# Output products with the tables stationary, and the stages behind the recurrence re-ordered, in a one-core trunk-and-MoE kernel

## What is computed

```
bu   = einsum(u, b)                      # u: tokens x 32 groups x 16 channels
h    = scan(a * h + bu)                  # complex, 64 states per group
y    = h_re @ c_re - h_im @ c_im + d * u # per group
y    = gelu(y);  y = y * sigmoid(y @ w_glu + b_glu)
mix  = concat([gated_mlp, y]) @ w_out;   x = x + gate1 * mix
h    = modulate(rms_norm(x));  group, expert = top-1 group, top-2 expert of h @ w_router
moe  = sum over the two experts of  gate * (silu(h @ w1) * (h @ w3)) @ w2
x    = x + gate2 * moe;                  out = rms_norm(x) * g_final
```

## Time and profile before

| what | us |
|---|---|
| median of three runs | 1870.66 |
| the profiled execution, its own time | 1870.08 |
| its span, first to last instruction | 1868.4 |

### The profile page before, as it was taken

How to read it: one execution, slowest core, us unless ns; L and a number is a source line. 1 busy time by engine, 2 the same in 40 slices (tenths; PEclk the granted TensorE clock), 3 DMA queues, 4 the chain that set the end, 5 groups by cost and what they waited for, 6 DMA issues and landing times. The chain is left out here.

```text
span 1868.4 us, 26204 instructions
## 1 busy us (share of the span) xinstructions
PE 1449.6 (78%) x6641; PEld 1086.6 (58%) x6642; DVE 1007.3 (54%) x2144; ACT 568.4 (30%) x976; POOL 701.0 (38%) x545
## 2 busy tenths in 40 slices
PE   3891899999859999398888886189999999994000
PEld 0140688888635666177777775168788887883000
DVE  3993756556355330335445553468555585761567
ACT  1121422323120000211111211068554485661232
POOL 0841223232115320023433333237443365563664
PEclk9996899999965555599999998589999999997555
DMA  4756311111181001634333342489976599985674
GB/s 117 267 181 219 113 68 45 67 57 61 36 164 40 18 6 69 233 115 166 136 135 135 149 149 73 155 276 372 359 270 244 207 370 363 325 313 184 215 276 161
DMA packets 165677, 322.78 MB, mean 173 GB/s; under 512 B 21677, under 2 KB 93421, under 8 KB 164952
## 3 DMA queue, kind: packets, MB, share of 16 engines
q1 hardware_dynamic: 150426, 276.20, 43.1%
q0 software_dynamic: 13664, 45.70, 7.1%
q10 hardware_dynamic: 1536, 0.26, 0.1%
HBM read 235.74 MB, written 86.39 MB: 172 GB/s over the span
## 5 line engine op out<-in xcount | busy, mean ns | idle before, releaser
L2022 POOL TENSOR_TENSOR down_lo<-expert_raw,down_hi (+1 forms) x64 | 157.1, 2476 | 180.9 <-ACT down_hi L2114 180.9
L2161 DVE TENSOR_TENSOR up_lo<-expert_raw,up_hi (+1 forms) x128 | 170.4, 1372 | 21.0 <-ACT up_hi L2109 20.2
L619 PE MATMUL ps_up<-up_hi,xT_hi 128*128 x400 | 161.8, 405 | 4.5 <-DVE up_lo L2161 2.9
L621 PE MATMUL ps_up<-up_hi,xT_lo 128*128 x400 | 157.2, 393 | 0.0
L620 PE MATMUL ps_up<-up_lo,xT_hi 128*128 x400 | 156.6, 392 | 0.0
L2109 ACT ACTIVATE up_hi<-expert_raw (+1 forms) x128 | 125.3, 1057 | 3.5 <-DMA expert_raw<-in_w 1.7
L619 PE MATMUL ps_out<-wout_hi,catT_hi 128*128 128x512 f32 (+1 forms) x272 | 109.0, 401 | 2.7 <-DVE catT_lo L1607 2.7
L621 PE MATMUL ps_out<-wout_hi,catT_lo 128*128 128x512 f32 (+1 forms) x272 | 107.5, 395 | 0.0
L620 PE MATMUL ps_out<-wout_lo,catT_hi 128*128 128x512 f32 (+1 forms) x272 | 107.4, 395 | 0.0
L448 PE MATMUL ps_ada<-wada,cT 128*9 128x512 f32 x192 | 87.7, 615 | 10.9 <-DMA wada<-in_w_ada 5.8
L782 POOL TENSOR_TENSOR v<-v,lng 128x512 f32<-128x512 f32 (+1 forms) x17 | 21.9, 1290 | 194.6 <-DVE v L931 194.6
(11 more groups left out here) (363 smaller groups left out, 3571.4 us busy)
## 6 DMA issues: line engine op xcount, KB each, us to landing
expert_raw<-in_w SPq DMA_DIRECT2D x96, 1024.0 KB
expert_rows<-yo SPq DMA_DIRECT2D x49, 512.0 KB
wada<-in_w_ada SPq DMA_DIRECT2D x12, 2048.0 KB
x<-in_x_prompt SPq DMA_DIRECT2D x32, 512.0 KB, 3.6
expert_rows<-blank SPq DMA_DIRECT2D x31, 512.0 KB, 4.1
x_rows<-x SPq DMA_DIRECT2D x16, 512.0 KB, 2.6
moe_in_rows<-h SPq DMA_DIRECT2D x16, 512.0 KB
x<-x_rows SPq DMA_DIRECT2D x16, 512.0 KB
```

The lines of the kernel that those rows point to most:

```text
L619: pe.matmul(out, left(0, k), right(0, k), start=k == 0, stop=False)
L621: last = pe.matmul(out, left(1, k), right(0, k), start=False, stop=k == n - 1)
L2022: pool.tensor_tensor(down_piece(down_lo, run, m), raw_piece(run, 2, m, 1), down_piece(down_hi, run, m).bitcast(F32), ALU.subtract).then_in ...
L2161: dve.tensor_tensor(up_piece(up_lo, run, m), raw_piece(run, m // 2, m % 2, KD // 2), up_piece(up_hi, run, m).bitcast(F32), ALU.subtract).t ...
```

## The change

`s5`. The output products swap their operands: the table is stationary and all 264 chunks of a group move, so a pair of groups takes six matmuls of 264 columns in place of what were, over the three sets of chunks, eighteen of 128. The result has steps and channels on the partitions; gelu writes it over the pair's inputs in `uT`; PE turns it back to token rows, four groups at a time and 128 chunks at a time, and ACT copies these. The sample chunks come first in `uT` now. Their outputs are gathered in one tile, turned, and stored with 32 small DMAs.

```
-                for m in range(4):
-                    for n in range(6 * m, 6 * m + 6):
-                        if m < 3 and n % 6 < 4:
-                            additions(4 * m + 4 + n % 6)
-                        outputs(n)
+                def outputs(k):
+                    if k == 0:
+                        pe.wait_ge(toep_in, 16 * Q)
+                    pe.wait_ge(h_ok, 2 * (k + 1))
+                    for g in range(2):
+                        if k > 0:
+                            pe.wait_ge(y_ok, 2 * (k - 1) + g + 1)
+                        pe.matmul(pB[:, g, 0:CH], toep[:, 2 * k + g, :], uT[:, 2 * k + g, :], start=True, stop=False)
+                    for h, m in ((h_re, S.m_re), (h_im, S.m_im)):
+                        for g in range(2):
+                            r = slice(g * ST, (g + 1) * ST)
+                            last = pe.matmul(pB[:, g, 0:CH], m[r, k, 1:9, :]..., h[r, k, 0:CH],
+                                             start=False, stop=h is h_im)
+                    last.then_inc(y_mm, 1)
+                def turn_back(m):
+                    pe.wait_ge(y_ok, 4 * m + 4)
+                    for t in range(2):
+                        if m > 0:
+                            pe.wait_ge(r_ok, 2 * (m - 1) + t + 1)
+                        for q in range(4):
+                            last = pe.transpose(pB[:, 2 + t, ...], uT[:, 4 * m + q, at[t]:at[t] + P], ident[:, :])
+                        last.then_inc(t_mm, 1)
+                for k in range(PAIRS):
+                    outputs(k)
+                    if k + 4 < PAIRS:
+                        additions(k + 4)
+                    if k >= 2 and k % 2 == 0:
+                        turn_back(k // 2 - 1)
+                turn_back(PAIRS // 2 - 1)
+                pe.wait_ge(y_ok, G + 1)
+                for i in range(2):
+                    pe.transpose(pB[:, i, 0:P], yT_samp[:, i * P:(i + 1) * P], ident[:, :]).then_inc(t_mm, 1)
...
+                for half in range(2):                       # SP
+                    cs = slice(half * DA // 2, (half + 1) * DA // 2)
+                    for t in range(2):
+                        sp.wait_ge(r_ok, 8 * half + 7 + t)
+                        sp.dma_start(y_rows[chunk[t]:chunk[t] + P, :, cs], rows[:, t, :, cs])
+                for i in range(2):
+                    sp.wait_ge(r_ok, PAIRS + i + 1)
+                    for g in range(G // 2):
+                        sp.dma_start(y_end[i, g, :, :, :], y_samp[g * NSEQ:(g + 1) * NSEQ, i, :]...)
...
+                for k in range(PAIRS):                      # ACT
+                    act.wait_ge(y_mm, k + 1)
+                    for g in range(2):
+                        act.activation(uT[:, 2 * k + g, :], pB[:, g, 0:CH], ACT.Gelu_apprx_tanh)
+                    if k >= 3 and k % 2 == 1:
+                        rows_back(k // 2 - 1)
```

```
@@ DVE step
                     if not last:
                         low_y(i + 1)
+                    if ranked:
+                        ranks(n - 2, 2)
                     gated(i, 0)
                     if not last:
                         bias_z(i + 1)
+                    if ranked:
+                        slots(n - 2, 2)
+                    if b == 1 and not (isinstance(n, int) and n == 0):
+                        select(n - 1, 2)
                     gated(i, 1)
-                    if b == 1 and not (isinstance(n, int) and n == 0):
-                        ranks(n - 1, 2)
...
-                    if b == 0 and not first:
-                        select(n - 1, 2)
-                    if b == 1 and not (isinstance(n, int) and n == 0):
-                        slots(n - 1, 2)
```

```
                     turn_x(b + 1, j + (t + 1) // AHEAD, (t + 1) % AHEAD)
+                    turn_hid(b - 1)
                     up_mm(b, t % 2, run_of(b))
                     down_mm(b - 1, run_of(b - 1))
-                    turn_hid(b)
```

```
                 def step(i, n, b):                          # POOL
-                    if within(i, NB - 1):
-                        if not (isinstance(i, int) and i == 0):
-                            pool.wait_ge(x_ok, i)
-                        gather(i + NB - 1, (b + NB - 1) % NB)
                     pool.wait_ge(two_ok, i + 1)
...
                     pool.tensor_tensor(yg[0:r, b, 1, :], yg[0:r, b, 1, :], g[0:r, :], ALU.mult)
+                    if i + AHEAD < NT:
+                        if i + AHEAD >= NB:
+                            pool.wait_ge(x_ok, i + AHEAD - NB + 1)
+                        gather(i + AHEAD)
```

More of the change, by code:

```diff
@@ L1075, in additions @@
                     last.then_inc(x_mm, 1)
[L1078 to L1082, removed]
-                        pe.wait_ge(toep_in, 16 * Q)
[L1084 to L1097, removed]
-                    last.then_inc(y_mm, 1)
@@ L1454, in step @@
                     if not first:
-                        logits(i - 1, NT if last else i + 2, n + b)
+                        logits(i - 1, NT if last else i + 2)
                 def rank(p, n):
@@ L1688, in step @@
                     first, last = isinstance(i, int) and i == 0, isinstance(i, int) and i == TP
+                    ranked = b == 0 and not (isinstance(n, int) and n < 2)
                     if last:
@@ L1704, in step @@
                         logits(i - 1, 1 - b)
+                    if last:
+                        select(7, 2)
                     dve.wait_ge(sq_ok, i + 1)
@@ L2156, in evac_x, with split_up @@
                                           xT_hi[:, par, ks, :].bitcast(F32), ALU.subtract).then_inc(x_d, 1)
-                def split_up(run, ms=range(4)):
-                    for m in ms:
+                def split_up(run):
+                    for m in range(4):
                         dve.wait_ge(up_h, 4 * run + m + 1)
@@ L2181, in step @@
                     evac_x(b + 1, prev)
[L2182 to L2187 removed]
+                    evac_hid(b - 1)
+                    split_next(dve, b, split_up)
+                    hidden(b, t % 2)
                     out(b - 1, AHEAD // 2 * j + (t - 1) // 2, prev)
[L2189 removed]
                 evac_x(0, 0)
@@ L2268, in step @@
                         sp.dma_start(o.y_prompt[0, ds(i * P, P), :], out[:, b, :]).then_inc(o_out[b], 16)
-                    if not isinstance(i, int) or i + NB < NT:
+                    if i + NB < NT:
                         load(i + NB, b)
-                tiles(sp, step)
+                tiles(step)
                 for b in range(NB):
@@ L2318, in _ @@
                 scale(1, 0, 1)
-                tiles(act, step)
+                tiles(step)
             @block.vector
@@ L2341, in norm @@
                     inv_sqrt(dve, c, rstd[0:r, :], ssq[0:r, b:b + 1], 1.0 / D, newton[0:r, 0:1], newton[0:r, 1:2])
[L2342 removed]
+                    if n > 0:
                         dve.wait_ge(o_out[b], 16 * n)
@@ L2357, in _ @@
                 residual(0, 0, 0)
-                tiles(dve, step, lambda i: c.at(INV * i))
+                tiles(step)
 _INS = ['x_prompt', 'x_sample', 'state_ssm_re', 'state_ssm_im', 'c_prompt', 'c_sample', 'w_ada', 'b_ada',
```

225 lines of the change are left out of this document (108 added, 117 removed).

## The result

The changed kernel takes 1723.1 us (median of 4 runs, 1722.4 to 1724.4) against 1871.3 for the kernel before: a ratio of 0.921, interval 0.920 to 0.923. Forecast were 1712 and the range 1668 to 1752. The profiled execution took 1722.7 us, its span is 1721.0, 147.4 less than before. (In the last batch of experiments three of eleven executions of the kernel before took 1802 to 1815 us at a mean granted clock of 0.87 to 0.88, the other eight 1869 to 1875 at 0.84; no trace of the three was kept, why they are shorter is open, and everything here is held against the longer ones.)

The account below looks back on a forecast made before the run. No engine was taken to bound the whole kernel; TensorE bounds s5 and experts, a chain between engines the final block. From 1870.1 us, less 80 (s5), 44 (mixout), 6 (experts) and 28 (final), came 1712, range 1668 to 1752.

Parts of the forecast that it names:

- s5, 80: s5: the next block starts at 681 in place of 761 us, 80 us gained, ends 39 and 96.
- the second rival: s5: the recurrence bounds, TensorE gets the high clock, outputs end at 646, SP issues at 0.33; total 1696 us; chance 0.2.
- the first rival: s5: products in the two row halves take turns, 6.2 us a pair, block 34 us later; total 1746 us; chance 0.15.
- mixout, 44: mixout: 37 us gained in the loop and 7 in the last tile, 44 us together.
- the deduction of 1.5 us a pair: mixout: 1.5 us per two tiles taken off a 5.8 us gain for delays after the reordering; net 5.3 us.
- the 24 DMAs, 0.3 us each, go out in the loop's last idle stretch of SP: mixout, last tile: the 24 DMAs for the samples' rows, 0.3 us each, fit into idle time of SP.
- experts, 6 gained: experts: TensorE's waits for hid shrink because hidden rows have a step more; 6 us gained, ends 3 and 11.
- used a turn of x later: experts: with four split parts ahead, hidden ends near the step's end and is used after TensorE's turn of x.
- final, 28: final block: opening the ring between engines and ending the wait for the samples' rows gains 28 us, ends 18 and 37.
- The third rival: final block: VectorE and GpSimd collide, 7.0 us a tile; total 1722 us; chance 0.2.
- I take 6.3: final block: 6.3 us a tile in place of 7.74, from limits of GpSimd 5.7, VectorE 5.4 and DMA 5.7.
- The fourth rival: s5: the samples' 32 small stores make the kernel slower, from 5.5 us a store; total 1885 us; chance 0.02.

Follow-up runs that it names:

- s_order: The changed kernel with the four 64-row products of s5 ordered by row half instead of taking the halves in turn: 1722.1 us.
- m_select_back: The changed kernel with only select in mixout put back behind the norm of the even step: 1769.2 us.
- e_hoist: The changed kernel with only TensorE's two register loads of the run numbers in experts moved ahead of the turn of x: 1717.6 us.
- e_three: The changed kernel with only the fourth part of VectorE's split in experts put behind hidden again: 1716.6 us.
- f_batch: The changed kernel with the final block's reciprocal root taken for two tiles at once, the product still on GpSimd: 1723.0 us.

## Why the prediction was right in its sum, and where its steps failed

The sum is near because errors went both ways: mixout gave 9 us more than forecast, experts and final together 21 less, and in s5 two errors of 8 us cancel. That part is luck.

**s5, 80 against 81.2: two errors that cancel.** The forecast had TensorE at the low clock until 655; it was the recurrence that bounded, and the outputs ended at 646.8, where the second rival had them (646). Its argument against that rival, that TensorE would be idle half of each pair and at the low level after idle, was wrong: idle for 2 to 3 us a pair it was mostly at the high one, a mean of 0.88. This gave 8 us. The stores took them: 0.80 each in place of 0.55, 25.75 us in place of 17.6. The trace before had the nearer row, ws_samp's 0.76; taking the mean of it and the cheapest issue seen (0.33, the final states' store) was the mistake. The overlap of the row halves, which the first rival doubted, was right (s_order). A drain between tiling modes, as the Trainium skill has it (TensorEngine Tiling (Array Packing), Tiling Modes, Key Properties), shows nowhere as an idle time of its own in the rows of a pair; the 0.1 us more for the toep products behind the additions (s_order) may be one of the three changes a pair, and with 2 us of slack a pair it would cost nothing.

**mixout, 44 against 53.4.** The wait for yT_lo went, as said. Forecast were seven pairs of tiles at 5.3 us; measured are six at 7.5, 45 us, and the seventh at nothing. In the six the step that failed is the deduction of 1.5 us a pair, for a second gating and logits that come late. Neither delay reached TensorE: it has no wait for logits, and a pair is 36.8 us of products. In the seventh it is "the 24 DMAs, 0.3 us each, go out in the loop's last idle stretch of SP": the price was right, but they held up the load of cat for tile 16, and TensorE waited 3.62 us for it and then ran at the low level. The loop gave 45 in place of 37, all by select's place (m_select_back). The last tile gave 8 where 7 were forecast: from its cat turns to the counts product 54.7 us passed before and 46.6 after.

**experts, 6 gained against 5.5 lost: wrong in sign.** The prediction read three waits for hid and gave hidden "a turn of x" of room. The step that failed is that with hidden "used a turn of x later" nothing is left to wait. For hid itself this held in most steps. But the prediction did not ask what stands behind the wait in TensorE's list, now ahead of the up product: the register load of the run, which begins only when hid is there (e_hoist). And in three steps hidden came later than the turn too, in the longest 2.4 us after the step's end (1196.26 against 1193.88): the turn gives 1.04, less than the fourth split part, 1.2 to 1.4, takes (e_three).

**final, 28 against 18.3.** The third rival, VectorE and GpSimd in each other's way at 7.0 a tile; measured 6.97. The step that failed is "I take 6.3", which took the best bound (5.4 of VectorE) as if the stall in the tail rows were an accident. In the kernel before, GpSimd's product mostly ran while VectorE stood waiting for it (2.35 idle); the change fills that idle time, and so puts VectorE's work beside the product in every tile. The rule of the Trainium skill (SBUF — State Buffer, Terms), that one engine holds the port pair while the other is blocked, agrees in kind: 1.66 us lost here, 2.1 and 2.7 in f_batch. In the trace the slow newton step ends with the product, as if held until then, and the product is longer, 3.26 in place of 2.57, where its span begins beside the residual. But three short instructions between the two ran at their usual 0.15 within the product's span.

**The fourth rival** did not come near: the stores cost 0.80, and 5.5 was needed.

## What to carry to other kernels

Before giving a waiting instruction more room, compare the room with all that the same change puts ahead of its producer, and look at what is queued behind the wait: a register load there begins only when the wait is over, and can cost time even where the data came in time for its own user. When a chain is opened so that VectorE becomes continuous, count GpSimd's elementwise work as a loss on VectorE too; moving it onto VectorE outright can be faster. Small stores at a barrier are priced by their number: merge them and send early what is ready early. And when loads are moved in an issuing engine's list, look at which load now stands behind them.

## What was not expected of the hardware

- Products in the two row halves run beside one another even where the list has both of one half first (s_order): four of 64 rows by 264 columns take 1.17 us in either order, two of 128 rows 1.08.
- Two engines that issue small DMAs at once got eight out in 6.3 us, 0.8 each, no faster than SyncE alone (0.69).
- TensorE was granted a mean clock of 0.88 in s5 while busy only 63 of 88 us; before, busy 199 of 220 us, most of it with products of 128 columns, it got 0.51. What decides between the levels is open.
